# Block attention of layer 1 issued as steps between the matmuls of its input projection

## The reference, cut to what matters

```
q, k, v, g = split(h @ w_in, [2048, 512, 512, 2048])      # 16 q heads, 4 kv heads of 128
# prompt: causal softmax(q k^T + alibi) v over its own 256 tokens
# sample: 8 sequences of 8 tokens, each with 2048 past tokens in 16 pages of 128 rows
k_past = k_pool[page_table]                               # a page: 128 x 512 float32, 256 KB
gate   = einsum(q, mean over each block of 256 keys)      # the 3 best of 8 blocks are kept
p      = softmax([scores of kept blocks, own scores])
o      = p @ [v_past, v_new]
x      = x + (o * silu(g)) @ w_out
```

## Time and profile before

| | before |
|---|---|
| median of 3 runs | 2283.45 us (2283.27 to 2285.18) |
| profiled execution: own time, span | 2286.8 us, 2285.2 us |
| PE, DVE, ACT, POOL busy, share of the span | 92%, 52%, 40%, 6% |
| HBM traffic | 348.29 MB read, 18.57 MB written |

### The profile page before, as it was taken

One profiled execution on the slowest core, in us unless ns is written; L12 is line 12 of the kernel. 1 busy time (PEld: TensorE's weight loads), 2 busy tenths in 40 slices (PEclk: granted clock), 3 DMA queues, 4 the chain that ended last, 5 costly groups with the idle time before them and its releaser, 6 DMA issues. The chain is left out here.

```text
span 2285.2 us, 39575 instructions
## 1 busy us (share of the span) xinstructions
PE 2100.0 (92%) x15842; PEld 1971.8 (86%) x15842; DVE 1186.4 (52%) x1818; ACT 914.4 (40%) x1425; POOL 141.4 (6%) x238
## 2 busy tenths in 40 slices
PE   7899999999999999999999878999977778599976
PEld 6799999999999999999999858999965555499956
DVE  5548666455564644565454446334426555445335
ACT  7435445243343523454333234223325555333323
POOL 0010000100101010001000000000000333100000
PEclk9999999999999999999999989999999999799988
DMA  8486554655646556555555714555523998555721
GB/s 231 137 207 172 141 148 127 164 143 146 169 122 173 135 157 191 149 146 155 149 148 148 248 52 111 149 151 152 152 74 120 353 339 296 143 148 166 228 72 47
DMA packets 516108, 369.05 MB, mean 161 GB/s; under 512 B 10627, under 2 KB 469740, under 8 KB 514958
## 3 DMA queue, kind: packets, MB, share of 16 engines
q1 hardware_dynamic: 498102, 305.62, 47.5%
q0 software_dynamic: 17856, 61.28, 8.3%
HBM read 348.29 MB, written 18.57 MB: 161 GB/s over the span
## 5 line engine op out<-in xcount | busy, mean ns | idle before, releaser
L120 ACT ACTIVATE w_high<-w_raw 128x2048 fp32r<-128x2048 f32 x232 | 443.9, 1913 | 899.9 <-PE bank L168 836.6
L125 DVE TENSOR_TENSOR w_low<-w_raw,w_high 128x2048 fp32r<-128x2048 f32 x232 | 531.4, 2290 | 268.3 <-ACT w_high L120 268.1
L164 PE MATMUL bank<-x_hi,w_high 128*128 128x320 f32 x1664 | 495.1, 312 | 0.0
L164 PE MATMUL bank<-x_lo,w_high 128*128 128x320 f32 x1664 | 489.5, 309 | 0.0
L164 PEld LDWEIGHTS bank<-x_hi,w_high 128*128 128x128 f32 x1664 | 312.3, 188 | 1.1
L164 PEld LDWEIGHTS bank<-x_lo,w_high 128*128 128x128 f32 x1664 | 312.5, 188 | 0.2
L168 PE MATMUL bank<-x_hi,w_low 128*128 128x320 f32 x1664 | 260.9, 309 | 0.0
L168 PEld LDWEIGHTS bank<-x_hi,w_low 128*128 128x128 f32 x1664 | 248.3, 188 | 0.0
L164 PE MATMUL bank<-xo_x_hi,w_high 128*128 128x320 f32 x640 | 189.8, 311 | 8.3 <-PEq L102 8.3
L164 PE MATMUL bank<-xo_x_lo,w_high 128*128 128x320 f32 x640 | 189.3, 310 | 0.0
L164 PEld LDWEIGHTS bank<-xo_x_hi,w_high 128*128 128x128 f32 x640 | 121.0, 189 | 8.6 <-issue 8.5
(11 more groups left out here) (409 smaller groups left out, 3506.6 us busy)
## 6 DMA issues: line engine op xcount, KB each, us to landing
w_raw<-in_ev_w_in SPq DMA_DIRECT2D x104, 1024.0 KB, 5.8
w_raw<-in_od_w_in SPq DMA_DIRECT2D x40, 1024.0 KB, 5.7
w_raw<-in_ev_w_out SPq DMA_DIRECT2D x32, 1024.0 KB, 5.8
key_pages<-in_cache_k SPq DMA_DIRECT2D x128, 256.0 KB, 4.8
value_pages<-in_cache_v POOLq DMA_DIRECT2D x128, 256.0 KB, 4.7
w_raw<-in_ca_w_kv SPq DMA_DIRECT2D x16, 1024.0 KB, 7.2
w_raw<-in_ca_w_q SPq DMA_DIRECT2D x16, 1024.0 KB, 5.6
w_raw<-in_od_w_out SPq DMA_DIRECT2D x16, 1024.0 KB, 5.9
```

The lines of the kernel that those rows point to most:

```text
L120: self.nc.scalar.activation(self.w_high[n % HI][:], self.w_raw[n % RAW][:], ACT.Copy).then_inc(self.w_hi, 1)
L125: self.nc.vector.tensor_tensor(self.w_low[n % RAW][:], self.w_raw[n % RAW][:], self.w_high[n % HI][:].bitcast(F32), ALU.subtract).then_inc ...
L164: e.nc.tensor.matmul(out, hi[:, k, cols], rhs(k)[part], start=(k == 0 and part == 0), stop=False)
```

## The change

Layer 1 is one block. All 40 tiles of the input projection and the 16 of the output projection are issued by `moba_layer`, and the attention is cut into steps that `weave` puts between the 48 matmuls of a tile: with n steps in a tile, 48 // (n + 1) matmuls stand before each step and the rest behind the last.

- The projection's tiles come in another order: k, q heads 0 to 7, v, q heads 8 to 15, gates.
- The eight sample units are no longer the eight sequences with four kv heads, but pairs of sequences with two kv heads. Unit U has the half tiles 24 + 6U to 24 + 6U + 11, so that the tail of one unit (turned probabilities "T", values "V", output rows "OT") stands beside the head of the next (keys turned "K", scores "S", exponentials "X").
- A page is read in two halves (1 KB of a row instead of 2 KB), for different units: 512 page loads instead of 256. The rings have 4 slots of 4 half pages for keys (SP) and as many for values (POOL).
- A prompt head has three steps at three successive odd half tiles: scores "pS", turned probabilities "pT", output "pO"; scores above the diagonal are left out.
- x is written to HBM at the start and read back at the end, since its place in SBUF holds the tables and probabilities meanwhile. The projections use 2 PSUM banks instead of 4.
- The ALiBi term of the past comes from a row of 256 key numbers and a column per block; the products with the SiLU gate are done per head during the gate tiles.

```
+def weave(pe, parts, steps, run):
+    count = 48 // (len(steps) + 1)
+    for step in steps:
+        for _ in range(count):
+            next(parts)
+        run(pe, step)
+    for _ in parts:
+        pass
...
+    BASE0, GAP = 24, 6
+    SC, TN, MI, PR = (2, 3), (4, 5), 6, 7
...
+    def steps(self, hs):
+        j, odd = divmod(hs, 2)
+        if odd and 1 <= j <= len(self.order) and 16 <= self.order[j - 1] < 24:
+            yield "rows", j - 1, 0
+        for U in range(8):
+            rel = hs - self.base(U)
+            if rel == 6:
+                yield "T", U, 0
+                yield "T", U, 1
+            if 7 <= rel <= 10:
+                yield "V", U, rel - 7
+                if rel < 10:
+                    yield "T", U, rel - 5
+                else:
+                    yield "V", U, 4
+            if rel == 11:
+                yield "OT", U, 0
+            if 1 <= rel <= 4:
+                yield "S", U, rel - 1
+            if rel == 4:
+                yield "S", U, 4
+            if 0 <= rel <= 3:
+                yield "K", U, rel
+        if odd:
+            for k, name in ((2, "pO"), (1, "pT"), (0, "pS")):
...
+    def pool(self, pool):
...
+        for i, (n, r) in enumerate((("k", self.krows), ("v", self.vrows))):
+            if i:
+                for Q in range(2):
+                    for bi in range(2):
+                        self.page(pool, "v", Q, bi, None)
+            pool.wait_ge(s["turn_out"], self.fill[("rows", self.order.index(19 + 4 * i), 0), 0] + 1)
+            pool.dma_start(d[f"{n}_prompt_o"][0, 0].rearrange("(t p) h c -> p t (h c)", p=128), r[:, 0:2, :]).then_inc(s["rows_stored"], 16)
+            pool.dma_start(d[f"{n}_sample_o"][0].rearrange("b t h c -> (b t) (h c)"), r[0:TSA, 2, :]).then_inc(s["rows_stored"], 16)
+        for Q in range(2, 32):
+            for bi in range(2):
+                self.page(pool, "v", Q, bi, (s["v_used"], Q - 1))
...
+    def turn_bank(self, pe, key):
+        f = self.fill[key]
+        if f >= 2:
+            pe.wait_ge(self.s["turn_out"], f - 1)
+        return self.e.bank[self.TN[f % 2]]
...
+        @block.scalar
+        def _(act):
+            for j in range(n):
+                e.high(act, m + j + AHEAD)
...
+                if j > 24:
+                    b.gate_scalar(act, j - 25)
...
+                for hs in (2 * j, 2 * j + 1):
+                    for step in b.steps(hs):
+                        b.scalar(act, step)
+                    for U in extra(hs, 5):
+                        b.scalar(act, ("X", U, 0))
...
+        @block.vector
+        def _(dve):
+            for j in range(n):
...
+                if j:
+                    b.evacuate(dve, j - 1)
+                e.low(dve, m + j + AHEAD)
+                if j > 25:
+                    b.gate_vector(dve, j - 26)
...
+                for hs in (2 * j, 2 * j + 1):
+                    for U in extra(hs, 0):
+                        b.vector(dve, ("Q", U, 0))
+                    if hs % 2 == 0 and 0 <= j - 17 < AH:
+                        b.vector(dve, ("pN", j - 17, 0))
+                    for U in extra(hs, 7):
+                        b.vector(dve, ("X", U, 0))
+                    for step in b.steps(hs):
+                        if step[0] in ("S", "pS"):
+                            b.vector(dve, step)
+                    for U in extra(hs, 10):
+                        b.vector(dve, ("O", U, 0))
...
-        p_od = Proj(e, columns(d["od_w_in"][0], wide(0, 40)))
-        p_odo = Proj(e, columns(d["od_w_out"][0], wide(0, 16)))
+        p_od = Proj(e, columns(d["od_w_in"][0], [128 * n for n in (*range(16, 20), *range(8), *range(20, 24), *range(8, 16), *range(24, 40))]), banks=(0, 1))
+        p_odo = Proj(e, columns(d["od_w_out"][0], wide(0, 16)), banks=(0, 1))
```

More of the change, by code:

```diff
@@ L65, in host_constants @@
     dist = np.where(q >= k, (k - q).astype(f), f(NEG)).astype(f).reshape(128, 512)
-    head, tok = np.arange(128) // TS, np.arange(128) % TS
-    past = (-slopes[head][:, None] * (PAST + tok[:, None] - np.arange(PAST)[None]).astype(f)).astype(f)
-    col = np.arange(64)
[L70 to L74, removed]
+    row = np.arange(128)
+    bi, hi, g, tok = row // 64, row // 32 % 2, row % 32 // TS, row % TS
+    keys = np.broadcast_to(np.arange(BLK).astype(f)[None], (128, BLK))
+    unit = np.zeros((128, 18), f)
+    own = np.full((128, 8, 64), NEG, f)
+    col = np.arange(64)
+    for hp in range(2):
+        slope = slopes[8 * hp + 4 * hi + g]
+        unit[:, hp] = slope
+        unit[:, 2 + 8 * hp:10 + 8 * hp] = -slope[:, None] * (PAST + tok[:, None] - BLK * np.arange(NBLK)[None]).astype(f)
+        for bp in range(4):
+            b = 2 * bp + bi[:, None]
+            d = tok[:, None] - col[None] % TS
+            own[:, 4 * hp + bp] = np.where((col[None] // TS == b) & (d >= 0), -slope[:, None] * d.astype(f), f(NEG))
     qmask = np.broadcast_to((col[None] // TS == np.arange(NB)[:, None]).astype(f).reshape(1, 512), (128, 512))
@@ L77, in host_constants @@
     sel3[np.arange(96), np.arange(96) % 32] = 1
-    return {"c_main": c, "c_dist": dist, "c_past": past, "c_own": own.reshape(128, 512),
+    return {"c_main": c, "c_dist": dist, "c_keys": np.ascontiguousarray(keys), "c_unit": unit, "c_own": own.reshape(128, 512),
             "c_qmask": np.ascontiguousarray(qmask), "c_sel3": sel3}
@@ L147, in bank, with parts @@
         return self.e.bank[self.e.tile_bank[self.tile0 + t]]
-    def tile(self, pe, t, rhs, ready=None):
+    def parts(self, pe, t, rhs, ready=None):
         e, n, g = self.e, self.slot0 + t // self.tps, self.tile0 + t
@@ L168, in tile @@
             m = e.nc.tensor.matmul(out, lo[:, k, cols], rhs(k)[0], start=False, stop=k == self.kch - 1)
-        m.then_inc(e.pe_tile, 1)
+            if k == self.kch - 1:
+                m.then_inc(e.pe_tile, 1)
+            yield
+    def tile(self, pe, t, rhs, ready=None):
+        for _ in self.parts(pe, t, rhs, ready):
+            pass
     def done(self, eng, t):
@@ L1830, in _ @@
                     v.tensor_tensor(g, g, o[:, :, TS * (b % 4):TS * (b % 4) + TS], ALU.mult).then_inc(s["out"], 1)
[L1833 to L1859, removed]
@@ L2186, in cross_attention, with residual_block @@
     return res
-def residual_block(e, label, p, res, chunks, y, split, first=False):
+def residual_block(e, label, p, res, chunks, y, split):
     nc = e.nc
```

763 lines of the change are left out of this document (467 added, 296 removed).

## The result

The changed kernel takes 2324.1 us, median of 4 (2322.8 to 2326.7), against 2283.4 us, median of 4 (2280.8 to 2285.2), for the kernel before: a ratio of 1.018, 95% interval 1.017 to 1.019. The direction held, and the stated range of 2250 to 2325 too, by 0.9 us. The likeliest case's own range, 2282 to 2316, did not hold, and neither did the size: I forecast 16 us more, and it is 41.

A forecast was written before the change was run, and what follows sets the result against it. PE bounds the projections and page loads the sample loop; layer 1 was to take 594 us work plus 107 waits plus 16 slow clock, 717 against 701, so 2283.45 + 16 = 2299 us, range 2250 to 2325.

The forecast's parts named there:

- Work at full clock: PE's work in layer 1 without waits: input projection 283.2, attention steps 198, output projection 112.6, together 594 us.
- Waits: PE's waits in layer 1: 38 + 46 + 15.5 + 2.6 + 4.5 + 1 = 107 us.
- OT: A unit's third tile: PE waits for `ms_orows` at the output rows, 5.9 us in a typical unit, 38 in sum.
- T and the first K: Next unit's first tile: PE waits for ACT's exponentials and copy of T0, 4.2 to 7.3 us, 46 in sum.
- the value page: Half tile 33: one wait of 15.5 us for value pages queued on POOL behind the stores of v rows.
- the start: Tile 1 of layer 1: the first "rows" step waits 2.6 us for the first evacuation.
- the end: Before the output projection: a wait of 4.5 us for evacuation, product and splits, in place of 12.78.
- the clock term: PE at 1.2 GHz after 17 waits, 1.7 us lost each: bounds 0 and 29, taken as 16 us.
- A unit of 58 to 61 us: Sign to look for in the changed trace: a unit's three tiles should take 58 to 61 us.
- Rival 1: Existing list order makes each of 15 unit waits 2.6 us shorter: 39 less, 2260 us; chance 0.25.
- Rival 2: Pages come late, 3 us missing in each of seven units, 21 in all: 2320 us; chance 0.15.
- The drain: About 1.38 us on top of ACT's table load, which the forecast rejected; with it 2303 instead of 2299 us.

The follow-up runs named there:

- The dummies: Changed kernel plus 387 matmuls that nobody reads, placed where PE waits in layer 1: 2298.6 us, ratio 1.007 to the kernel before.
- both lists by due time: Changed kernel with ACT and DVE lists reordered by what PE needs next, and value pages issued ahead of v-row stores: 2226.8 us, ratio 0.975 to the kernel before.

## Why the prediction was right and wrong

- *Work at full clock.* 594 forecast, 591 by the line. If the projections take the 283 and 113 of the forecast, the steps are 195 and not 198. Right within 2 per cent: my price of K steps, 1.29 for two fills, had a wait of 0.25 us in it, 8 us over 32 K steps that are no work; without them it is 586.
- *Waits.* 107 forecast, 106.6 measured: each named wait stood in its place, but the sum met this well by luck. The terms that I named came out shorter. OT is 31.0 against 38: 4.9 to 5.3 us in four units where I had 5.9 and 6.3, 3.7 and 4.5 in two (5.2 and 5.4), 2.5 in the last (3). T and the first K are 38.5 (22.5 + 2.7 + 13.3) against 46, the value page 14.0 against 15.5, the start 2.5 against 2.6, the end 4.5 as forecast. These make 90.5. Waits that my sum did not have made up for the rest: 10.8 for copies of keys (8 of it counted as work above), 3.3 for a second value page in the last unit, 2.0 for an evacuation of q.
- ***The step that failed is the clock term: "I take 16", with bounds of 0 and 29.*** By the line it is 0.36 x 116 = 42 us. With 42 for 16 the forecast would be 2325, against 2324.1. The dummies test this term on its own: they took 106 us of slow time away (38 us by the line), gave 14 back as work beyond the waits, and the kernel gained 25.6.
- Why the bound itself was too low: it counted one slow stretch of 3.4 us, 1.7 us lost, for each of 17 waits. There are 20 stretches, 116 / 20 = 5.8 us long in the mean, and each costs 0.36 x 5.8 = 2.1. Three of the seven waits at T0, which I had lumped with K, are followed by one of their own before the wait at K. The earlier trace rows shows a pause that was followed by one slow stretch, and I took that one for the rule, and then only 16 of its 29. The trace of before had the evidence against it: 61 us in 8 stretches, three of them of 10 us and more. The stated range held, by 0.9 us, only because it had the second rival's price in it.
- *A unit of 58 to 61 us.* From one OT to the next 59.8, 62.5, 61.6, 65.4, 65.0 and 58.9 us. By the line 3 to 5 us of each are the clock, where my 58 to 61 had about 1.
- *Rival 1* (shorter waits by the order as written): no. It wanted 2.6 us less at each of the 15 unit waits; they came out 1.0 us shorter (69.5 against 84), and the small waits took that back. But waits of this size were there to be won with another order: two edits that each move one step in one list gave 38 and 35 us, and both lists by due time give 2227.
- *Rival 2* (pages late in each unit): no. No key page was waited for, and the page's DMA part shows the smaller loads landing in less than the 4.7 us that I took. Those on POOL start 1.15 us apart (median), where I took 1.29 (and 1802.49 - 1801.19 is 1.30):

```profile
value_pages<-in_cache_v POOLq DMA_DIRECT2D x256, 128.0 KB, 3.2
key_pages<-in_cache_k SPq DMA_DIRECT2D x256, 128.0 KB, 2.9
```

- *The drain*, which the Trainium skill, page ScalarE: Activation LUTs, section What ACT_TABLE_LOAD costs, adds to a load: not seen in the trace, and the run without SiLU does not ask for it.

## What to carry to other kernels

When work is woven into another engine's stream, each helper engine's list decides: an operation that is ready and short (`ms_orows`, 0.34 us) must not stand behind 8 us of others that nobody waits for yet. Price a wait on PE as its length plus the slow clock behind it: here 106.6 us of waits brought 42 us more, so a microsecond of wait cost 1.4 in the mean. And take a mean over all such places in the trace, not one example, for a term that is counted 17 times.

## What was not expected of the hardware

Pauses of about 2 us are at times followed by slow time, and at times not. In the kernel before, four of the seven waits of 2.00 us for exponentials have a slow stretch that begins within 2 us of their end, and three have none. In the changed kernel, PE's timeline at T0 and the window behind it:

```profile
1734.93 0.79 PE L2162 MATMUL bank<-const,ms_p 128*128 128x128 f32 x4 [2.05 <-ACT ms_p L2240]
```

```profile
1735.30:1738.70 3.40, 3.40 (x15) 0.50 0.62 168
```

In the kernel by due time two waits at K of nearly the same length, and the windows behind each:

```profile
1583.70 1.06 PE L2137 MATMUL bank<-const,key_pages 128*128 128x128 f32 x8 [2.14 <-ACT ms_pt L2246]
...
1732.41 0.85 PE L2137 MATMUL bank<-const,key_pages 128*128 128x128 f32 x5 [2.13 <-ACT ms_pt L2246]
```

```profile
1583.70:1587.10 3.40, 3.05 (x36) 1.00 1.09 311
...
1733.00:1736.40 3.40, 3.40 (x17) 0.51 0.17 50
```

The first costs its length, the second costs the clock too; of the seven waits at K there, two do. With 0.36 us for each us at 1.2 GHz in this mixed stream, a kernel gained 25.6 us from 387 matmuls that compute nothing. What decides between a pause that costs clock and one that does not stays open: no run here varied the length of a single pause.
